# A hybrid decoder step on one core: stick-breaking sums of the prompt from a softplus in two rounded parts

## The reference

```python
z = q . k * 64**-0.5 + bias[head]            # [query, key]
valid = k_pos < q_pos                        # strictly causal
log_stay = where(valid, log_sigmoid(-z), 0)  # = -softplus(z)
after = reverse_cumsum(log_stay, keys) - log_stay
w = where(valid, exp(log_sigmoid(z) + after), 0)
o = w @ v
```

## Time and profile before

| | |
|---|---|
| median of 3 runs | 1368.58 us |
| profiled execution, its own time | 1368.12 us |
| its span, first to last instruction | 1366.4 us |
| mean granted clock of TensorE | 0.954 |
| TensorE busy | 1257.4 us (92%) |
| VectorE busy | 592.7 us (43%) |
| ScalarE busy | 416.4 us (30%) |
| GpSimd busy | 140.4 us (10%) |

### The profile page before, as it was taken

One profiled execution on the slowest core, in us unless ns is written; L12 is line 12 of the kernel. 1 busy time (PEld: TensorE's weight loads), 2 busy tenths in 40 slices (PEclk: granted clock), 3 DMA queues, 4 the chain that ended last, 5 costly groups with the idle time before them and its releaser, 6 DMA issues.

```text
span 1366.4 us, 22443 instructions
## 1 busy us (share of the span) xinstructions
PE 1257.4 (92%) x9540; PEld 1191.4 (87%) x9540; DVE 592.7 (43%) x642; ACT 416.4 (30%) x483; POOL 140.4 (10%) x157
## 2 busy tenths in 40 slices
PE   7999999999995999999897697799999999999883
PEld 6999999999995899997674287699999999999883
DVE  5444422344328376552554333644442234432844
ACT  5322222222224233112552344332222222222532
POOL 7000000000013121110000002300000000001311
PEclk9999999999998999999988589899999999999997
DMA  5222122222230212122331021022222222223111
GB/s 190 93 92 84 60 97 98 93 92 70 61 116 18 93 63 78 49 97 78 110 108 62 31 79 64 30 93 92 84 65 97 93 93 92 69 67 112 62 32 66
DMA packets 39774, 110.09 MB, mean 81 GB/s; under 512 B 4962, under 2 KB 4978, under 8 KB 39586
## 3 DMA queue, kind: packets, MB, share of 16 engines
q1 hardware_dynamic: 37906, 103.13, 22.7%
q0 software_dynamic: 1232, 5.01, 1.0%
q10 hardware_dynamic: 576, 1.08, 0.2%
HBM read 103.57 MB, written 5.64 MB: 80 GB/s over the span
## 4 chain that ended last, share of the span: by engine, by line
PE 84%; DVE 9%; ACT 5%; issue 1%; POOL 0%; DMA 0%; POOLq 0%; ACTq 0%; DVEq 0%
PE PS L463 74%; DVE work L1239 2%; DVE x L1251 2%; DVE a_lo L1230 1%; PE PS L630 1%; DVE w_lo L1224 1%; ACT w_hi L901 1%; PE PS L476 1%; PE PS L776 1%; PE PS L657 1%; PE PS L767 1%; PE PS L856 1%; PE PS L687 0%; PE PS L799 0%; PE PS L754 0%
## 5 line engine op out<-in xcount | busy, mean ns | idle before, releaser
L463 PE MATMUL PS<-a_hi,w_hi 128*128 128x272 f32 x2064 | 437.4, 294 | 45.5 <-DVE a_lo L1230 22.2
L463 PE MATMUL PS<-a_lo,w_hi 128*128 128x272 f32 x2064 | 432.0, 291 | 0.0
L463 PE MATMUL PS<-a_hi,w_lo 128*128 128x272 f32 x2064 | 429.9, 290 | 0.0
L463 PEld LDWEIGHTS PS<-a_hi,w_hi 128*128 128x128 f32 x2064 | 327.2, 190 | 56.1 <-issue 30.1
L463 PEld LDWEIGHTS PS<-a_hi,w_lo 128*128 128x128 f32 x2064 | 328.2, 190 | 0.5
L463 PEld LDWEIGHTS PS<-a_lo,w_hi 128*128 128x128 f32 x2064 | 327.9, 190 | 0.5
L1224 DVE TENSOR_TENSOR w_lo<-raw,w_hi 128x2048 fp32r<-128x2048 f32 (+3 forms) x107 | 204.2, 1909 | 235.3 <-ACT w_hi L901 235.3
L901 ACT ACTIVATE w_hi<-raw 128x2048 fp32r<-128x2048 f32 (+3 forms) x107 | 168.0, 1570 | 75.8 <-PE PS L463 75.8
L463 PE MATMUL PS<-h_hi,w_hi 128*128 128x272 f32 x704 | 145.9, 289 | 0.0
L463 PE MATMUL PS<-h_lo,w_hi 128*128 128x272 f32 x704 | 145.6, 288 | 0.0
L463 PE MATMUL PS<-h_hi,w_lo 128*128 128x272 f32 x704 | 144.4, 286 | 0.0
(11 more groups left out here) (311 smaller groups left out, 961.0 us busy)
## 6 DMA issues: line engine op xcount, KB each, us to landing
raw<-in_f_in SPq DMA_DIRECT2D x86, 512.0 KB, 4.4
raw<-in_f_out SPq DMA_DIRECT2D x32, 384.0 KB, 3.4
raw<-in_f_out SPq DMA_DIRECT2D x32, 320.0 KB, 3.0
raw<-in_w_rest SPq DMA_DIRECT2D x40, 256.0 KB, 2.8
k_pages<-in_cache_sb_k SPq DMA_DIRECT2D x16, 256.0 KB, 2.9
raw<-in_w_out SPq DMA_DIRECT2D x8, 512.0 KB, 4.7
raw<-in_ple_w_gate SPq DMA_DIRECT2D x8, 512.0 KB, 4.4
x<-in_x SPq DMA_DIRECT2D x8, 272.0 KB, 7.2
```

The costliest lines, as they stand in the source:

```text
L463: last = mm(PS[0:width, 4 * quad + 2 * c + half, 0:HALF], wt[:, slot, cols], act[:, k, half * HALF:(half + 1) * HALF], start=(k == 0 and n ...
```

## The change

The softplus of each head is divided into a high and a low rounded part, and each of the nine sums becomes two rounded products, one with each part. The masks of ones and the triangle get rounded copies, made once. The high part (`high`) is two ScalarE copies, of 512 and 768 columns, into memory that is idle by then; the low part (`low`) is two VectorE subtractions of the same widths, written over the softplus itself. The sums wait for the low part instead of the softplus.

```diff
+        sp_low = [w_lo[:, spare_at, 0:1280], w_extra[:, 0:1280]]
+        sp_high = [(h_row[:, 0:512], h_row[:, 512:1280]), (h_row[:, 1280:1792], w_hi[:, spare_at, 1280:SLOT])]
+        ones_r, tri_r = sum_r[:, 0, :], sum_r[:, 1, :]
...
             def prompt_sums(h):
-                s_ = sb_s[h % 2]
-                pe.wait_ge(sig["sp_ready"], h + 1)
+                parts = [sp_low[h % 2][:, a_:b_] for a_, b_ in ((0, 512), (512, 1280))]
+                pe.wait_ge(sig["sp_low_ready"], h + 1)
                 pe.wait_ge(sig["d_ready"], h)
-                mm(PS[:, 4, :], tri[:], s_[:, 0:512], start=True, stop=True)
...
+                def both(out, mask, at_, n, start=False, stop=False):
+                    for i, (diag, rest) in enumerate((sp_high[h % 2], parts)):
+                        src = diag[:, at_:at_ + n] if at_ < 512 else rest[:, at_ - 512:at_ - 512 + n]
+                        last = mm(out, mask, src, start=start and i == 0, stop=stop and i == 1)
+                    return last
+                both(PS[:, 4, :], tri_r, 0, 512, start=True, stop=True)
...
+            def high(n):                                   # ScalarE
+                act.wait_ge(sig["sp_ready"], n + 1)
+                if n >= 2:
+                    act.wait_ge(sig["c_full"], n - 1)
+                fn(sp_high[n % 2][0], sb_s[n % 2][:, 0:512], ACT.Copy)
+                fn(sp_high[n % 2][1], sb_s[n % 2][:, 512:1280], ACT.Copy).then_inc(sig["sp_high_ready"], 1)
...
             log_part(1, sb_s[1])
+            act.wait_ge(sig["og_out"], GLA_HEADS)
+            fn(ones_r, ones[:], ACT.Copy)
+            fn(tri_r, tri[:], ACT.Copy).then_inc(sig["ones_r_made"], 1)
+            high(0)
             logits(1, 0)
+            high(1)
             logits(1, 1)
...
                 weight(2 * p + 1, sb_z[(2 * p + 1) % 6])
+                if p + 1 < pairs:
+                    high(2 * p + 2)
                 if p + 2 < pairs:
                     logits(p + 2, 0)
                 if p + 1 < pairs:
                     log_part(2 * p + 3, sb_s[1])
                 if p + 2 < pairs:
                     logits(p + 2, 1)
+                if p + 1 < pairs:
+                    high(2 * p + 3)
...
+            def low(n):                                    # VectorE
+                dve.wait_ge(sig["sp_high_ready"], n + 1)
+                for first, high_ in zip((0, 512), sp_high[n % 2]):
+                    end = 512 if first == 0 else 1280
+                    ins = v.tensor_tensor(sp_low[n % 2][:, first:end], sb_s[n % 2][:, first:end], high_.bitcast(F32),
+                                          ALU.subtract)
+                ins.then_inc(sig["sp_low_ready"], 1)
...
             softplus(1, sb_z[1], sb_s[1])
+            low(0)
             masked(1)
+            low(1)
...
                 exponents(2 * p + 1)
                 if p + 1 < pairs:
+                    low(2 * p + 2)
                     magnitudes(2 * p + 3)
                 if p + 2 < pairs:
                     masked(p + 2)
                 if p + 1 < pairs:
                     softplus(2 * p + 3, sb_z[(2 * p + 3) % 6], sb_s[1])
+                    low(2 * p + 3)
```

More of the change, by code:

```diff
@@ L167, in build @@
             pass
+        with nc.sbuf_tensor("w_extra", [P, 3 * 1280], F32R) as w_extra:
+            pass
         extra = sb("extra", [P, 3 * 1280])
@@ L177, in build @@
             w_hold = sb("w_hold", [P, 768], F32, s)
+            sum_r = sb("sum_r", [P, 2, P], F32R, s)
         hold_a = sb("hold_a", [P, 2 * KD * T])
@@ L210, in build @@
         sb_s = [scratch(spare[1], 0, [P, 1280]), scratch(extra_flat, 0, [P, 1280])]
+        spare_at = (at["out"][0] + 1) % 2
+        sp_low = [w_lo[:, spare_at, 0:1280], w_extra[:, 0:1280]]
+        h_row = h_hi[:].rearrange("p k t -> p (k t)")
+        sp_high = [(h_row[:, 0:512], h_row[:, 512:1280]), (h_row[:, 1280:1792], w_hi[:, spare_at, 1280:SLOT])]
+        ones_r, tri_r = sum_r[:, 0, :], sum_r[:, 1, :]
         x_flat = x[:].rearrange("p k a t -> p (k a t)")
@@ L276, in build @@
             og_full og_out wide_out on_full on_out sn_full sn_decayed sn_out
-            gv_full gv_out so_out q_zero diag_half qz_ready k_stored v_stored nat_stored state_stored new_stored m_mid pg_ready pg_sig pg_out gg_ready m_sq m_norm m_ready rows_out""".split()
+            gv_full gv_out so_out q_zero diag_half qz_ready k_stored v_stored nat_stored state_stored new_stored m_mid pg_ready pg_sig pg_out gg_ready m_sq m_norm m_ready rows_out sp_high_ready sp_low_ready ones_r_made""".split()
         sig = {n: sem(n) for n in names}
@@ L771, in prompt_sums @@
             def prompt_sums(h):
-                s_ = sb_s[h % 2]
-                pe.wait_ge(sig["sp_ready"], h + 1)
+                parts = [sp_low[h % 2][:, a_:b_] for a_, b_ in ((0, 512), (512, 1280))]
+                pe.wait_ge(sig["sp_low_ready"], h + 1)
                 pe.wait_ge(sig["d_ready"], h)
-                mm(PS[:, 4, :], tri[:], s_[:, 0:512], start=True, stop=True)
[L777 to L784, removed]
+                def both(out, mask, at_, n, start=False, stop=False):
[4 more added lines that the diff above has]
+                both(PS[:, 4, :], tri_r, 0, 512, start=True, stop=True)
+                both(PS[:, 5, 0:384], tri_r, 512, 384, start=True)
+                both(PS[:, 5, 0:384], ones_r, 128, 384)
+                both(PS[:, 5, 128:384], ones_r, 896, 256)
+                both(PS[:, 5, 256:384], ones_r, 1152, 128, stop=True)
+                both(PS[:, 6, 0:384], tri_r, 896, 384, start=True)
+                both(PS[:, 6, 0:256], ones_r, 256, 256)
+                both(PS[:, 6, 128:256], ones_r, 1152, 128)
+                both(PS[:, 6, 256:384], ones_r, 384, 128, stop=True).then_inc(sig["c_full"], 1)
             def prompt_out(p):
```

## The result

The changed kernel takes 1382.37 us (median of 4 runs, 1380.8 to 1384.4) against 1369.8 of the kernel before beside it; the ratio is 1.0092 (1.0071 to 1.0113), slower by 0.92%. The profiled execution of before took 1368.12, next to the fastest of the runs beside (1368.08), and that of after (1384.40) was the slowest of its four, so the two traces differ by 16.3 us and the medians by 12.6. What follows compares traces; 3.7 us of their difference is spread between runs.

What follows compares the result with a forecast made beforehand. The prediction took VectorE and ScalarE handing to each other in the prompt's stick-breaking sums as the limit there: 1.9 + 6.8 + 4.9 + 1.7 - 1.1 = 14.2 on 1368.12, forecast 1382.5 us, range 1379 to 1385.5 (0.70).

Steps and rivals of the forecast that it cites:

- Exponents of head 0: Start of the loop: first sums start 4.5 us late but take 3.6 instead of 6.25, so these exponents come 1.9 late.
- the walk: Step-by-step count of the prompt's stick-breaking stretch through the engine queues, from first sums to head 7's exponents: +14.2 us.
- The two stops: Per pair: 4.35 us between head 2p+1's exponents and the next magnitudes, 3.0 ahead of the next pair's exponents.
- First pair: Exponents of head 0 to head 2: 21.65 us plus a wait for head 2's logits, 24.2 against 17.4, +6.8.
- Second: Exponents of head 2 to head 4: 21.65 + 1.3 + 4.2 with the weight division, 27.1 against 22.2, +4.9.
- Third pair: Exponents of head 4 to head 6: 21.65 us against 20.0, +1.7.
- Head 7: Its sums wait for head 6's exponents, 1.55, then take 3.6: 5.2 us against 6.3 before, -1.1.
- The price of the rounded sums: One head's high and low products, 5120 columns: 2.55 us at 2.4 GHz, 4.5 at 1.2; 3.6 taken for all.
- Rival B: Narrow rounded products cost more: a head's sums about 5.0 us on average, +18.3, 1386.5 us; chance 0.13.
- Rival C: A division costs less than the rows say: 2.0 instead of 2.95 us at 7 stops, 1375.8 us; chance 0.10.
- Rival A: TensorE was the limit and the division hides: -12.4, 1356 us, or 1362 if half is had; chance 0.05.
- The 2.1 us that I gave to the rule: All sums at 1.2 GHz because of the gaps between them: +16.3, 1384.4 us, instead of +14.2.

Runs made afterwards that it cites:

- div_plain: The changed kernel with the nine sums plain fp32 products again, reading the low part alone, the division kept; 1389.13 us.
- high_first: The changed kernel with one move on ScalarE: head 2p+2's high copy ahead of head 2p+1's weight Exp; 1377.07 us.
- round_free: The changed kernel without the division: softplus written rounded at once, both rounded products of each sum read it; 1364.28 us.
- all_warm: The changed kernel with high copies ahead of weight Exps, low parts and pair 1's weight division behind magnitudes, idle-time products (24; 34, 44, 34); 1368.13 us.
- warm: The changed kernel with idle-time TensorE products: 24 plain ahead of the first sums, then 50, 66, 46 rounded in pairs 0, 1, 2; 1382.31 us.
- all_late: The changed kernel with high copies ahead of weight Exps, low parts behind magnitudes, pair 1's weight division behind both, no idle-time products; 1371.37 us.
- all_late_warm: all_late with idle-time TensorE products: 24 ahead of the first sums, 34 each in pairs 0 and 2, none in pair 1; 1365.81 us.

## Why the prediction was right

The forecast was 1382.5, slower; measured 1382.4. Its mechanism, the division in series with the loop of VectorE and ScalarE, is what div_plain and high_first showed. Step by step, from the table above:

- Exponents of head 0: predicted +1.9, measured +2.2. The first sums ran wholly at the lower clock (5.17), where I took 3.6 for all sums; they started 1.2 earlier than the walk had them, counted from the copy (17.4 against 18.6).
- The two stops: predicted 4.35 and 3.0, measured 4.07 and 2.91. Copies took 0.61 and 0.83, overlapping, 1.35 together (1.40 taken); the low part 1.56 (1.55).
- First pair: predicted 24.2, measured 23.7 (670.65 to 694.37). Second: 27.1, measured 26.6. Both right within 0.5: of the waits for TensorE before, only the one for head 2's logits was left in them. (The walk's own terms for that wait, 669.55 + 2.6 + 1.3, make 673.45 and not 673.65.)
- Third pair: predicted 21.65, measured 24.3. This is the term that was mis-sized. I had counted no wait for TensorE there. The sums of head 4 took 5.17 at the lower clock and the products for the next logits and pages behind them 5.48 (1.31 + 4.17); in the first pair there were 16 page products, here 32, and the clock fell from 1.00 to 0.50 again under them (720 to 724). So the magnitudes of head 6 waited 2.06 (724.53) and the exponents of head 5 0.90 (731.06) for the sums of head 5.
- Head 7: predicted 5.2, measured 4.6; its sums ran at the full clock (2.87 instead of 3.6).
- TensorE's busy time: predicted 15 to 20 less. The old stretch shows 14.9 less, but part of the work has moved out of it; over the whole execution it is 7.8 less. The 15 to 20 did not fit the walk either: 3.6 for each head makes 28.8 against the 41.4 before, 12.6 less, and four heads took about 5.2.

In the trace that makes 15.5 in the stretch where the walk had 14.2; the medians differ by 12.6. The third pair was 2.6 too low, the other two and head 7 were 1.6 too high together, and the difference of the two traces is 3.7 over that of the medians. So the closeness to 0.1 us is luck; the sign and the size within some 3 us are not.

The price of the rounded sums was too low at either clock: 2.87 measured against 2.55, and 5.17 against 4.5. Of the 0.3 at the full clock, the narrow products explain about half: three pairs of 128 columns, each 0.05 over the price by columns. The same trace shows most of the rest: the product of 384 columns behind a narrow pair took 0.23 up to the next start instead of 0.18 (674.98 to 675.21), and the first product of a head 0.31 instead of 0.24 (746.89 to 747.20). Rival B is refuted (2.87, where it asked for more than 3.3); its factor of four was 3.6 by the rows (384 columns take 0.64 plain in two passes, 0.18 rounded). Rival C is refuted too: the stops cost what the rows said. Rival A failed as the prediction said it would, at the start of head 2's sums (685.99, 4.2 behind the exponents of head 1). Its price of 17 us for the shorter sums was wrong as well: round_free got 5.1.

The rule of the Trainium skill, in "TensorE: Matmul & The Clock Gate", section "Why this matters for your kernels", that gaps between bursts bring back the lower rate, held for the even heads: after 5.8 to 8.0 us without a product the sums of heads 0, 2, 4 and 6 ran at a granted clock of 0.50. The prediction's reading that it would put all sums at the lower clock was wrong. The sums of heads 1 and 3 stood behind other products, with no gap, and ran at 1.00, and those of head 7 did so after a wait of 2.33 (744.57 to 746.89). Nor is a gap needed: in all_warm the clock fell while TensorE was busy with page products. The 2.1 us that I gave to the rule (1.8 by the two terms of 0.9 that the walk names, at the first exponents and at head 7) are not confirmed: warm shows 2.6 in one trace and nothing in the medians. Between all_late and all_late_warm the filling is worth 5.6.

## What to carry to other kernels

Work that was put between two engines that hand to each other cost about its full time at each hand-over (4.07 together with the weight Exp that it stood behind, and 2.91; the rows of these instructions add up to 4.2 and 2.9), though both looked half idle by their shares (50% each). Count the loop of hand-overs and the waits in it, and look in each queue at what the new instruction stands behind. Shortening what those engines wait for paid only as far as they waited, and TensorE's clock after the longer gaps took part of it back. Before an order is judged, give both versions the same helps: here the best changed kernel and the kernel before, each with helps, end level.

## What the runs showed of the hardware

Idle-time products can keep the clock up: with 24 plain ones of 128 columns ahead, the first sums took 2.87 instead of 5.17. But they sit in TensorE's queue like any other work: in all_warm 44 of them took 7.40, partly at 0.50, and the sums behind them started 7.8 later, counted from the copy of the natural values, than in all_late_warm, which has none there.

The clock also fell without a gap, each time while TensorE was in products of 8 columns: in all_warm from 1.00 at 696.5 to 0.50 at 700, in the changed kernel from 1.00 at 720 to 0.50 at 722.5.

Of two rounded products of 128 columns in a row the second started 0.06 after the first, and the product behind them 0.11 after the second. Where two such pairs follow each other, the products of the second pair started 0.11 apart as well (675.79, 675.90). Weight loads start 0.11 apart there too (674.81, 674.92, 675.03), which points at them as the limit; that was not tried.
